# Operands of the down projection transferred straight to their places, last pair summed in the second down quad, and three additions to the residual per quad moved from VectorE to GpSimd

## The reference, cut to what matters

```
x = x + 0.5 * swiglu(rmsnorm(x, p['g_ffn1']), p['w1_gate'], p['w1_up'], p['w1_down'])
...                                   # LRU, sliding-window attention, cross attention
x = x + 0.5 * swiglu(rmsnorm(x, p['g_ffn2']), p['w2_gate'], p['w2_up'], p['w2_down'])

def swiglu(x, w_gate, w_up, w_down):
    return (jax.nn.silu(x @ w_gate) * (x @ w_up)) @ w_down
```

## Time and profile before

| what | value |
|---|---|
| median of 3 runs | 2219.37 us (2211.6 to 2219.86) |
| profiled execution, its own time | 2222.69 us |
| span of its trace | 2220.8 us |
| PE busy | 2128.5 us, 96% |
| DVE busy | 1590.0 us, 72% |
| ACT busy | 823.7 us, 37% |
| POOL busy | 509.9 us, 23% |
| mean granted TensorE clock | 0.987 of full speed |

### The profile page before, as it was taken

The page is one execution under the profiler, slowest core; times in us unless marked ns, Lnnn a source line. Parts: engine busy times, 40 slices in busy tenths (PEclk is TensorE's granted clock), DMA queues, the critical chain, the costliest instruction groups (busy, mean ns, idle before and its releaser), DMA issues. The chain is left out here.

```text
span 2220.8 us, 39530 instructions
## 1 busy us (share of the span) xinstructions
PE 2128.5 (96%) x15452; PEld 2013.8 (91%) x15452; DVE 1590.0 (72%) x2295; ACT 823.7 (37%) x1396; POOL 509.9 (23%) x499
## 2 busy tenths in 40 slices
PE   6899999998999999999999999998999999989998
PEld 5899999998998888878898887988999999989987
DVE  7977878877779578899526155368778778766884
ACT  6423333334434324557412034154233233344332
POOL 1011111210000256778535321520121111100002
PEclk9999999999999999999999999999999999999999
DMA  3123233248524121143411062312233233475322
GB/s 140 63 108 132 97 143 118 107 167 321 191 92 163 71 96 38 59 151 102 159 38 59 19 246 85 127 40 78 94 132 130 110 132 119 179 283 194 130 103 81
DMA packets 82296, 271.93 MB, mean 122 GB/s; under 512 B 9096, under 2 KB 21384, under 8 KB 68616
## 3 DMA queue, kind: packets, MB, share of 16 engines
q1 hardware_dynamic: 79232, 267.01, 32.9%
q10 hardware_dynamic: 2951, 3.35, 0.5%
HBM read 191.22 MB, written 76.32 MB: 120 GB/s over the span
## 5 line engine op out<-in xcount | busy, mean ns | idle before, releaser
L922 PE MATMUL ps<-act_hi,op_hi 128*128 128x272 f32 x1712 | 496.8, 290 | 26.4 <-issue 13.0
L923 PE MATMUL ps<-act_lo,op_hi 128*128 128x272 f32 x1712 | 497.4, 291 | 0.0
L924 PE MATMUL ps<-act_hi,op_lo 128*128 128x272 f32 x1712 | 496.7, 290 | 0.0
L922 PE MATMUL ps<-t_hi,op_hi 128*128 128x272 f32 x1392 | 404.4, 290 | 8.4 <-DVE op_lo L2156 7.1
L924 PE MATMUL ps<-t_hi,op_lo 128*128 128x272 f32 x1392 | 403.3, 290 | 0.0
L923 PE MATMUL ps<-t_lo,op_hi 128*128 128x272 f32 x1392 | 403.3, 290 | 0.0
L922 PEld LDWEIGHTS ps<-act_hi,op_hi 128*128 128x128 f32 x1712 | 326.1, 190 | 30.0 <-issue 28.2
L1607 ACT ACTIVATE op_hi<-sums 128x512 fp32r<-128x512 f32 (+2 forms) x232 | 138.9, 599 | 526.6 <-DVE sums L2162 325.3
L923 PEld LDWEIGHTS ps<-act_lo,op_hi 128*128 128x128 f32 x1712 | 325.7, 190 | 0.0
L924 PEld LDWEIGHTS ps<-act_hi,op_lo 128*128 128x128 f32 x1712 | 325.5, 190 | 0.0
L922 PE MATMUL ps<-act_hi,w_hi 128*128 128x288 f32 (+1 forms) x864 | 290.4, 336 | 7.3 <-DVE act_lo L2082 2.0
(11 more groups left out here) (355 smaller groups left out, 3991.9 us busy)
## 6 DMA issues: line engine op xcount, KB each, us to landing
raw_gu<-in_w_gu SPq DMA_DIRECT2D x40, 1024.0 KB, 6.8
w_raw<-in_w_plain SPq DMA_DIRECT2D x54, 512.0 KB, 3.3
hid<-hid_o SPq DMA_DIRECT2D x20, 1088.0 KB, 4.9
hid_t<-hid_o SPq DMA_DIRECT2D x18, 1088.0 KB, 4.1
hid_h<-sum_hi SPq DMA_DIRECT2D x18, 544.0 KB, 5.2
x<-x_keep SPq DMA_DIRECT2D x16, 544.0 KB, 7.5
raw_dq<-in_w_dq SPq DMA_DIRECT2D x8, 1024.0 KB, 9.2
ck_T<-in_ck SPq DMA_DIRECT2D x8, 1024.0 KB, 7.0
```

What stands on the lines that cost most here:

```text
L922: pe.matmul(out, wh, ah, start=(first and n == 0), stop=False, skip_group_check=goes_on)
L923: pe.matmul(out, wh, al, start=False, stop=False, skip_group_check=goes_on)
L924: ins = pe.matmul(out, wl, ah, start=False, stop=end, skip_group_check=goes_on)
```

## The change

1. The hi and the sum of parts 3, 4 and 5 go by DMA to the tiles that PE reads. The copies on ACT that wrote them there again (L1637, L1639: six for each group) are gone, and PE waits for the transfers themselves (`refilled`). ACT's copy for part 6 stands after product 3.
2. Pair 9 and pair 10 change places: pair 9 is now one of those done plainly, and needs no sums, and pair 10 belongs to the last group. Its sums are made later: POOL's four after its store has landed, ahead of all of POOL's additions to x; ACT's hi after product 2 of D1; DVE's subtraction after product 5 of D1; SP's stores behind the weights of D2, ahead of rows 6, 7, 0, 1 of x and of the weights of D3.
3. `add_part` is POOL's. The counts that DVE and ACT wait for (`x_added`) stay.

```diff
-LAST_PAIRS = (0, 10)
+PAIR_AT = (0, 1, 2, 3, 4, 5, 6, 7, 8, 10, 9)
+LAST_PAIRS = (0, 9)
...
+        end_off = (X0 + KH * ROW + 2 * ROW + 4 * TH, X0 + KH * ROW + 2 * ROW)
+        end_hi = [at(f"end_hi{i}", [P, 1, w], end_off[i], F32R) for i, w in enumerate((T, TH))]
...
-                    sp.dma_start(operand(j, kh)[2], hidden_part(j, p0, p0 + kh)).then_inc(f[f"mv_in{j % 3}"], 16)
+                    hi, lo, raw = operand(j, kh)
+                    to = lo.bitcast(F32) if j in SPLIT_OPS else raw
+                    sp.dma_start(to, hidden_part(j, p0, p0 + kh)).then_inc(f[f"mv_in{j % 3}"], 16)
                     if j in SPLIT_OPS:
-                        sp.dma_start(operand_hi(j, kh), t_in["hid_h"][:, p0:p0 + kh, j - SPLIT_OPS[0], :])\
+                        sp.dma_start(hi.bitcast(F32), t_in["hid_h"][:, p0:p0 + kh, j - SPLIT_OPS[0], :])\
...
-                load_moving(f, 0, range(2))
-                sp.wait_ge(f["t_out"], upto(f, "t_out", 16 * OUTS * (SUMMED - 1) + 16))
-                store_highs(f, SUMMED)
-                load_moving(f, 0, range(2, 3))
+                sp.wait_ge(f["t_out"], upto(f, "t_out", 16 * OUTS * (SUMMED - 1)))
+                x_again(1, 0)
                 load_down(f, dq, QUADS + 1)
-                sp.wait_ge(f["t_out"], upto(f, "t_out", 16 * OUTS * SUMMED))
-                x_again(1, 0)
-                load_moving(f, 0, range(3, 6))
+                load_moving(f, 0, range(6))
...
                 load_down(f, dq, QUADS + 2)
-                for m in range(2):
-                    x_again(3, m)
-                sp.wait_ge(f["hid_out"], upto(f, "hid_out", 16 * (FI + 1)))
-                for m in range(2):
-                    x_again(0, m)
+                store_sums(f, PAIR_AT.index(FI - 1), upto(f, "sum_lo", 2 * SUMMED))
+                store_highs(f, PAIR_AT.index(FI - 1), end_hi)
+                sp.wait_ge(f["t_out"], upto(f, "t_out", 16 * OUTS * SUMMED))
+                for q in (3, 0):
+                    for m in range(2):
+                        x_again(q, m)
...
             def hidden_sums(f):
 
-                with pool.Fori(1, SUMMED + 1) as i:
+                with pool.Fori(1, SUMMED) as i:
                     pool.wait_ge(f["hid_out"], i * 16 + upto(f, "hid_out", 32))
                     pair_sums(f, i * 4 + upto(f, "t_made", -4))
+                pool.wait_ge(f["hid_out"], upto(f, "hid_out", 16 * (FI + 1)))
+                pair_sums(f, upto(f, "t_made", 4 * (SUMMED - 1)))
+
+            def add_part(f, u, m, h, part, evicted):
+
+                g, q, _ = down_of(u.n)
+                if g == 0:
+                    pool.wait_ge(*x_back_again(f, q, 1 if u.n == QUADS and m == 0 else 2))
+                pool.wait_ge(f["quad_ev"], u.count(EVICTS, upto(f, "quad_ev", evicted)))
+                row = half(x[:, 2 * q + m, :], h)
+                pool.tensor_tensor(row, row, part[:, :, :], ALU.add).then_inc(f["x_added"], 1)
+
+            def down_quads(f):
+
+                for v in range(QUADS, ALL_QUADS):
+                    u = Quad(v)
+                    add_part(f, u, 0, 1, u2, U2)
+                    add_part(f, u, 1, 0, p1, U3)
+                    add_part(f, u, 1, 1, p1, C22)
...
-                        pe.wait_ge(f["mv_hi"], upto(f, "mv_hi", HI_MADE * u.group() + hi_made(j)))
+                        pe.wait_ge(*refilled(f, u.group(), j))
...
-                act.activation(hi, operand_hi(j, kh) if j in SPLIT_OPS else raw, ACT.Copy).then_inc(f["mv_hi"], 1)
-                if j in SPLIT_OPS:
-                    act.activation(lo, raw, ACT.Copy).then_inc(f["mv_hi"], 1)
+                hi, _, raw = operand(j, DOWN_GROUPS[g][1])
+                act.activation(hi, raw, ACT.Copy).then_inc(f["mv_hi"], 1)
...
-                    if u.ends_before_group() and 2 <= j < 6:
+                    if u.ends_before_group() and 2 <= j < 5:
                         refill_hi(f, u.group() + 1, j - 2)
+                    if n == QUADS + 1 and j == 2:
+                        sums_hi(f, u, end_hi)
...
-                add_part(1, 1, p1, C22)
+                if u.n == QUADS + 1:
+                    sums_lo(f, u, end_hi)
```

More of the change, by code:

```diff
@@ L79 @@
 DOWN_PAIRS = (1, 2, 3, 0)
-LAST_PAIRS = (0, 10)
+PAIR_AT = (0, 1, 2, 3, 4, 5, 6, 7, 8, 10, 9)
+LAST_PAIRS = (0, 9)
 LAST_K = [2 * p + i for p in LAST_PAIRS for i in range(2)]
 LAST_ROWS = (2, 3, 6, 7)
-assert sorted([p for p0, kh in DOWN_GROUPS for p in range(p0, p0 + kh)] + list(LAST_PAIRS)) == list(range(FI))
+assert sorted([p for p0, kh in DOWN_GROUPS for p in range(p0, p0 + kh)] + [PAIR_AT.index(p) for p in LAST_PAIRS]) == list(range(FI))
 SPLIT_OPS = (3, 4, 5)
@@ L468, in refilled @@
             return f[f"mv_in{i}"], upto(f, f"mv_in{i}", g * MV_IN[i] + landed)
-        def hi_made(j):
-            return sum(2 if v in SPLIT_OPS else 1 for v in range(j + 1))
         def x_back_again(f, q, rows=2):
@@ L602, in store_sums, with store_highs @@
                              hid_o[:, :, :].rearrange("p m n -> p (m n)")).then_inc(f["t_out"], 16)
[L604 to L605 removed]
+            def store_highs(f, i, high=sum_hi):
+                sp.dma_start(t_in["hid_h"][:, i, 0:2, :].rearrange("p a n -> p (a n)"), high[0][:, 0, :].bitcast(F32))\
                   .then_inc(f["t_out"], 16)
[L607 removed]
+                sp.dma_start(t_in["hid_h"][:, i, 2, :], high[1][:, 0, :].bitcast(F32)).then_inc(f["t_out"], 16)
             def store_hidden(f, i, v):
@@ L843, in _ @@
             hidden_sums(f)
+            down_quads(f)
             pool.wait_ge(f["quad_mm"], STEPS * ALL_QUADS)
@@ L1616, in quad_silu, with sums_hi @@
                 act.activation(sg[:, m, h, :, :], sg[:, m, h, :, :], ACT.Silu).then_inc(f["silu"], 1)
-            def sums_hi(f, u):
-                act.wait_ge(f["t_made"], u.turn(4, upto(f, "t_made", 0)))
-                act.activation(sum_hi[0][:, :, :], hid_o[:, 0:1, :], ACT.Copy).then_inc(f["sum_hi"], 1)
-                act.activation(sum_hi[1][:, :, :], hid_o[:, 1:2, 0:TH], ACT.Copy).then_inc(f["sum_hi"], 1)
+            def sums_hi(f, u, high=sum_hi):
+                made = 4 * SUMMED if u.down() else 0
+                act.wait_ge(f["t_made"], upto(f, "t_made", made) if made else u.turn(4, upto(f, "t_made", 0)))
+                act.activation(high[0][:, :, :], hid_o[:, 0:1, :], ACT.Copy).then_inc(f["sum_hi"], 1)
+                act.activation(high[1][:, :, :], hid_o[:, 1:2, 0:TH], ACT.Copy).then_inc(f["sum_hi"], 1)
             def keep_p1(f, u):
@@ L1648, in quad @@
                         keep_p1(f, u)
-                    if u.opens_group() and j < 3:
-                        refill_hi(f, u.group(), 4 + j)
+                    if u.opens_group() and j == 3:
+                        refill_hi(f, u.group(), 6)
                     if u.opens_down() and j == 0:
@@ L1659, in quad @@
                         quad_hi(f, n, 1 - s, j)
-                    if gate and j == 4 and u.later():
+                    if gate and j == 4 and u.i is not None:
                         sums_hi(f, u)
@@ L2191, in quad_part @@
                 dve.wait_ge(f["silu"], u.turn(4, upto(f, "silu", 2 * NC + n + 1)))
-                if n == 0 and (u.i is not None or u.n > 1):
-                    early = 16 * (OUTS - 1) if u.next().opens_down() else 0
-                    dve.wait_ge(f["t_out"], u.turn(16 * OUTS, upto(f, "t_out", -early)))
+                if n == 0 and u.next().opens_down():
+                    dve.wait_ge(f["hid_out"], upto(f, "hid_out", 16 * FI))
+                elif n == 0 and u.i is not None:
+                    dve.wait_ge(f["t_out"], u.turn(16 * OUTS, upto(f, "t_out", 0)))
                 dve.tensor_tensor(half(hid_o[:, m, :], h), to, sg[:, m, h, :, :], ALU.mult).then_inc(f["hid_f"], 1)
@@ L2232, in quad @@
                 quad_part(f, u, s, C21, lambda: low(4))
-                if s == 0 and u.later():
+                if s == 0 and u.i is not None:
                     sums_lo(f, u)
@@ L2319, in add_bank @@
                                                     op0=ALU.mult, op1=ALU.add).then_inc(f["quad_ev"], 1)
-                def add_part(m, h, part, evicted):
-                    dve.wait_ge(f["quad_ev"], u.count(EVICTS, upto(f, "quad_ev", evicted)))
-                    row = half(x[:, 2 * q + m, :], h)
-                    dve.tensor_tensor(row, row, part[:, :, :], ALU.add).then_inc(f["x_added"], 1)
                 def with_p1(to):
```

29 lines of the change are left out of this document (10 added, 19 removed).

## The result

| | median | lowest to highest | runs |
|---|---|---|---|
| before | 2219.61 us | 2211.6 to 2220.58 | 4 |
| after | 2243.4 us | 2241.34 to 2245.43 | 4 |

The ratio is 1.0111, with a 95% interval of 1.0091 to 1.013: the change makes the kernel slower by 1.1%. The forecast was 2239 us, with a range of 2218 to 2250. The medians are 23.8 us apart, where 19.4 were forecast.

A forecast was written before the change was run, and what follows sets the result against it. PE, busy 96% of the span, was taken as the bound, so only its idle or half-clock time counts. Terms of +9.7 us per layer, twice +19.4, gave 2239 us against the median, range 2218 to 2250.

The forecast's parts named there:

- D0: First down quad: wait for p goes, product 6 waits 5.2 us for part 6, half clock adds 1.2; -3.9 us a layer.
- D1: Second down quad: POOL's seven instructions, in turns with DVE, make p late for product 2; +2.9 us a layer.
- D2: Third down quad: late weights of D3 delay U2; PE waits 7.7 us at product 4, half clock 1.9; +9.6 a layer.
- openings and last group: Openings of groups 2 and 3, -0.4 us; additions on POOL holding full DVE in the last group, +1.5; per layer.
- A: Rival: POOL does not hold D1, D2 loses least (5.1 us idle, 1.6 half clock); 2224 us, chance 0.15.
- B: Rival: weights of D3 land before S + 10.0, in time for DVE's sums in D2; 2219.6 us, chance 0.08.
- C: Rival: D0 gives back nearly all (-6.6), POOL holds nothing, D2 costs 5.1; faster, 2209 us, chance 0.14.
- D: Rival: shared port makes last group heavy, +4 a layer, and D2 costs its upper bound, 10.3 + 1.9; 2249 us, chance 0.11.

The follow-up runs named there:

- e10: Kernel of e6 with ACT's six copies per group kept, so only the later sums of pair 10 remain of the change: 2215.33 us, ratio 0.9986.
- e6: Kernel after, with the weights of D3 issued ahead of the last sums' stores and the additions back on DVE: 2211.42 us, ratio 0.9961.
- e1: Kernel after, with the weights of D3 issued ahead of the stores of pair 10's sums: 2219.71 us, ratio 1.0002.
- e9: Kernel of e5, with the additions of the last group (D8 to D11) on DVE, those of D0 to D7 on POOL: 2214.25 us, ratio 0.9971.
- e7: Kernel of e5, with each POOL addition cut to one column of each 272, a bound and no version: 2208.01 us, ratio 0.9951.
- e2: Kernel after, with the three additions per quad back on DVE at their old places: 2235.95 us, ratio 1.0064.
- e5: Kernel after, with D3's weights ahead of the last sums' stores and POOL's additions of D0 ahead of its four differences: 2215.78 us, ratio 0.9979.

## Why the prediction was right, point by point

By the prediction's terms, from the rows above (idle time and lost clock, 6 us less an eighth of the matmuls). Before, D0 lost 6.3 + 1.6 + 1.6 = 9.5 us in the first layer and 10.0 in the second. For the last line, the waits of PE that remain after D2 in the views of both kernels were added: 8.0 and 6.8 us before, 8.2 and 7.6 after.

| term | forecast | first layer | second layer |
|---|---|---|---|
| D0 | -3.9 | 3.5 + 1.5 - 9.5 = -4.5 | 4.0 + 2.7 - 10.0 = -3.3 |
| D1 | +2.9 | 2.1 + 1.5 = +3.6 | 0.9 + 0.1 = +1.0 |
| D2 | +9.6 | 10.8 + 2.5 = +13.3 | 8.6 + 2.2 = +10.8 |
| openings and last group | +1.1 | +0.2 | +0.8 |
| sum | +9.7 | +12.6 | +9.3 |

The sums are 21.9 us together. By the starts of products the down quads of the two layers took 12.9 and 10.6 us longer than before, 23.4 together (last table), beside 23.8 between the medians. The 1.5 us that the terms lack are half clock in the second group of the second layer, which no list of waits shows. PE waits there for act_lo in both layers, 1.86 and 1.88 us, and the 6 us behind it differ (first layer, second layer):

```profile
626.90:632.90 6.00, 5.96 (x48) 5.99 (x49) 5.95 (x10) 1.92 (x5) 1.10 (x1) 1.00 0.01 3
2074.50:2080.50 6.00, 6.00 (x36) 6.00 (x37) 5.95 (x10) 1.35 (x3) 1.05 (x1) 0.72 0.01 3
```

The time forecast came near by terms that missed in both directions, as follows.

*D0.* The chain held: no wait for p, product 6 waits for act_lo. Part 6 landed at 1973.0 (issued at 1960.1, 12.9 us). D0's product 1 started 10.9 us later than before because of the first layer, so this is 1962.1 on the clock of before, where I had 1963.0. PE started product 6 at 1977.7, 4.7 us after the landing (5.0). Half clock cost more than the 1.2 us that I took: 1.5 and 2.7. In the second layer a wait 1.2 us shorter than forecast (4.0, not 5.2) and half clock 1.5 us longer nearly cancel, so the term is closer than its parts. e10 shows a thing that my text implied and did not say: what D0 gives back comes of the traffic, not of the copies.

*D1.* The mechanism was right: POOL's seven instructions ran without a break after the landing, in turns with DVE, and PE waited for p. DVE's timeline beside them shows six instructions in a row that take 2.5 to 2.7 times as long as alone (two of them, then an operation that reads PSUM and isn't held):

```profile
1977.46 1.83 DVE L2167 TENSOR_TENSOR op_lo<-raw_dq,op_hi 128x512 fp32r<-128x512 f32 x1
...
1986.38 1.74 DVE L2173 TENSOR_TENSOR sums<-raw_dq 128x512 f32<-128x512 f32 x1
1988.04 0.71 DVE L2331 SCALAR_TENSOR_TENSOR x<-ps,x 128x544 f32<-128x544 f32 x1
```

The size was not right. I had 13.5 us for the chain from the end of part 6's lo, with turns of 1.36 + 0.6 = 1.96 us; DVE's instructions start 1.76 us apart, and from the end of the lo (1977.5) to the end of the chain (1989.35) it is 11.8 us. On the clock of before the chain ended at 1978.5, where I had 1981.0: 0.9 us come of the earlier landing and 1.7 of the faster turns. PE was due at product 2 at 1978.8 (1978.2). So the wait of the second layer was 2 us shorter than forecast, mainly because the chain was shorter. In the first layer it was 2.1, and a half clock stretch of its own (1.5), which I had not counted, made up for that: that the term fits there is luck.

*D2.* The largest term was mis-sized, low by 3.7 and 1.2 us. Of its links in the second layer, from the start of D2, S = 2005.6: the first store was issued at S + 2.1, where I had S + 0.8; the landing was seen 6.1 us later, where I had 6.8; the loads took 2024.3 - 2013.8 = 10.5 us (9.9); sums and U2 2.1. In the first layer the store and its landing took the same times, and the loads 12.6 us, from 563.92 to 576.53, past my bound of 11.3; most of the 3.7 us is this link. The other link that failed is the step "Product 5 of D1 ends at S - 3.0. DVE then does C21". Product 5 did end there, at 2002.65, but DVE was still at two operations of 128x512 that took 1.51 and 1.73 us beside POOL's additions of D1 (2000.71 to 2003.84), and C21 started at S - 1.3, in both layers. In e6, with the additions on DVE, C21 starts 0.4 us after product 5 ends and not 1.7. So part 3 of the change lengthened this chain too, and my sum had no term for that. The order of the chain and its releasers were as forecast, and e1 shows that they made the wait.

*Openings and last group.* +1.1 forecast, 0.2 and 0.8 by the waits. By the starts of products the stretch from product 6 of D2 to product 6 of D7 took 1.8 us less than before in the first layer and 1.4 more in the second (the half clock above), and the rest, to the first plain pair, 2.3 and 0.6 more. My +1.5 a layer for the additions in the last group lies near the mean of these two, and above the 1.0 a layer that the traces of all runs give (e9). What the additions cost in all with the orders mended is 4.4 us by e6, and e7 bounds it at 7.8. The Trainium skill ("Perfetto Trace Analysis", section "Optimizing Scalar/DVE Operations") says that such a move "might not help"; read as no effect, this is not what the runs show: it made the kernel slower, by e2 and by e6.

*The rivals.* A fell with the turns in D1 and with a wait in D2 of 8.6 and 10.8 us, where it had 5.1. B fell with the weights of D3, whose sums DVE started at S + 18.7, where S + 10.0 decided. Its time, 2219.6 us, is nearly that of e1 (2219.71), by luck: it takes 19.2 us off a forecast of 2238.8, and e1 took 23.7 off 2243.4. C would have needed D0 to give back nearly all; e5 and e6, with D2 out of the way, give back 4.5 and 8.8 us in two layers. D was half right: its 12.2 us for D2 lies between the measured 13.3 and 10.8, closer than my 9.6, but its +4 in the last group was not there. The measured time lies about midway between forecast and D.

## What to carry to other kernels

Before a small store with a wait is put into a queue that is issued in order, list what stands behind it and when each of those is needed: here 6.1 us of waiting for stores, and four loads that nobody wanted yet, made the whole net loss, and one line moved took it away. A copy that ends a wait is worth removing only as far as the next link; read the landing of the transfer behind it first. And work moved from DVE to POOL is priced by what it does to DVE's own instructions while it runs, in the stages where something waits for them.

## What the runs showed of the hardware

- DVE's operations on two SBUF tiles and GpSimd's take turns, one for one: in D1 of after DVE's start 1.76 us apart, and POOL's additions 1.75. Beside GpSimd a subtraction of 128x512 took 1.83 us, where it took 0.68 alone; a difference of GpSimd took 1.68 and an addition 1.80, where an addition took 1.33 alone; the one difference that started during a DVE operation of 2.43 us took 3.08. DVE's operations with an operand in PSUM stayed at 0.71 us. The Trainium skill ("SBUF — State Buffer", section "SBUF: two separate sides") states an exclusive lock on a shared pair of ports for a DVE operation with two SBUF inputs; the trace agrees.
- What an idle stretch of PE costs afterwards doesn't follow its length in these rows. After 0.90 us idle 47 matmuls ran in the next 6 us, after 1.86 us 48, after 1.88 us 36, after 2.10 us 36, after 3.50 us 36, after 3.98 us 26, after 8.63 us 30, after 10.78 us 28. The six stretches with fewer than 47 cost 1.5 to 2.7 us each, and no row here says what decides between them.
